# A spatial gate with one bias product per pair of heads, inverse steps placed among the vector engine's other work, and row turns one tile later

## The reference, cut to what matters

```python
def spatial_gating(u, v, ln_g, ln_b, w_s, b_s):
    v = layer_norm(v, ln_g, ln_b).reshape(b_, n, A_CHUNK, A_HEADS, HEAD_DIM)
    w = jnp.where(mask, w_s, 0.0)                    # 4 heads, 128 x 128, lower triangle
    z = jnp.einsum('hij,bnjhd->bnihd', w, v) + b_s.T[:, :, None]
    return u * z.reshape(b_, t, A_WIDTH_2)

def gated_delta_rule(q, k, v, log_g, beta):          # 8 heads, chunks
    sol = lax.linalg.triangular_solve(eye + lower, rhs, left_side=True, lower=True, unit_diagonal=True)
    ...                                              # then a recurrence over the chunks

def gla_chunked(q, k, v, log_a):                     # 4 heads, chunks of 64
    o_intra = jnp.einsum('bhnij,bhnjv->bhniv', p_intra, v)
    ...                                              # plus a state carried from chunk to chunk
```

## Time and profile before

| | us |
|---|---|
| median of 3 runs (3999.33 to 4000.17) | 3999.43 |
| the profiled execution | 3998.43 |
| its span, first to last instruction | 3996.6 |
| PE busy | 3807.0 (95% of the span) |
| DVE busy | 2082.7 (52%) |
| ACT busy | 1382.5 (35%) |

### The profile page before, as it was taken

One profiled execution on the slowest core, in us unless ns is written; L12 is line 12 of the kernel. 1 busy time (PEld: TensorE's weight loads), 2 busy tenths in 40 slices (PEclk: granted clock), 3 DMA queues, 4 the chain that ended last, 5 costly groups with the idle time before them and its releaser, 6 DMA issues.

```text
span 3996.6 us, 44618 instructions
## 1 busy us (share of the span) xinstructions
PE 3807.0 (95%) x18516; PEld 3137.8 (79%) x18516; DVE 2082.7 (52%) x3673; ACT 1382.5 (35%) x2100; POOL 86.4 (2%) x164
## 2 busy tenths in 40 slices
PE   8998989999999999999999988999999999899998
PEld 5975489999986688888887766888788877577886
DVE  5936757644456543333347467433633374756335
ACT  5434533212356432322226424222322255233222
POOL 0100001111000000000000000000000000000000
PEclk9998999999999999999999958999999999679999
DMA  6410014433320122232222201222222222002222
GB/s 225 151 43 1 1 43 132 125 127 127 103 69 22 43 95 95 99 109 100 96 95 81 78 1 43 95 95 97 85 100 95 96 84 81 15 33 85 95 99 81
DMA packets 92877, 333.35 MB, mean 83 GB/s; under 512 B 11362, under 2 KB 11522, under 8 KB 92420
## 3 DMA queue, kind: packets, MB, share of 16 engines
q1 hardware_dynamic: 77040, 278.10, 20.2%
q0 software_dynamic: 12800, 41.95, 3.4%
q10 hardware_dynamic: 2836, 10.44, 0.7%
HBM read 328.35 MB, written 2.10 MB: 83 GB/s over the span
## 4 chain that ended last, share of the span: by engine, by line
PE 89%; DVE 5%; ACT 5%; issue 1%; DMA 0%; DVEq 0%; ACTq 0%; SPq 0%
PE PS L511 73%; PE PS L1078 2%; PE PS L513 2%; PE PS L1063 1%; PE PS L1094 1%; PE PS L1066 1%; PE PS L1424 1%; PE PS L944 0%; PE PS L2372 0%; PE PS L2168 0%; PE PS L1395 0%; PE PS L716 0%; PE PS L1995 0%; ACT XH L891 0%; DVE H_r L680 0%
## 5 line engine op out<-in xcount | busy, mean ns | idle before, releaser
L511 PE MATMUL PS<-arena_r,ring_hi 128*128 128x512 f32 (+1 forms) x6224 | 2106.0, 377 | 71.2 <-DVE H_r L680 70.1
L511 PE MATMUL PS<-arena_r,ring_r 128*128 128x512 f32 (+1 forms) x4752 | 1781.4, 375 | 0.0
L511 PEld LDWEIGHTS PS<-arena_r,ring_hi 128*128 128x128 f32 x6224 | 1168.4, 189 | 253.3 <-DVE H_r L680 61.9
L511 PE MATMUL PS<-H_r,ring_hi 128*128 128x512 f32 (+1 forms) x3280 | 1231.3, 375 | 0.0
L511 PEld LDWEIGHTS PS<-arena_r,ring_r 128*128 128x128 f32 x4752 | 897.6, 189 | 131.9
L380 DVE TENSOR_TENSOR ring_r<-ring,ring_hi 128x1024 fp32r<-128x1024 f32 x514 | 627.7, 1222 | 660.5 <-ACT ring_hi L371 660.0
L371 ACT ACTIVATE ring_hi<-ring 128x1024 fp32r<-128x1024 f32 x514 | 541.9, 1056 | 875.3 <-DMA ring<-weights_dram 867.5
L511 PEld LDWEIGHTS PS<-H_r,ring_hi 128*128 128x128 f32 x3280 | 622.9, 190 | 95.5 <-issue 3.1
L1654 ACT ACTIVATE arena<-PS 128x512 f32<-128x512 f32 x88 | 52.7, 598 | 532.6 <-PE PS L511 532.6
L1232 DVE SCALAR_TENSOR_TENSOR XH<-PS,mods,XH 128x256 f32<-128x256 f32 (+1 forms) x144 | 68.5, 524 | 237.3 <-PE PS L511 237.3
L1658 DVE SCALAR_TENSOR_TENSOR arena<-arena,PS 128x512 f32<-128x512 f32 x88 | 60.5, 688 | 225.8 <-PE PS L511 225.8
(11 more groups left out here) (370 smaller groups left out, 3164.2 us busy)
## 6 DMA issues: line engine op xcount, KB each, us to landing
ring<-weights_dram SPq DMA_DIRECT2D x526, 512.0 KB, 3.2
rstd<-ada_later_dram POOLq DMA_DIRECT2D x54, 256.0 KB, 2.9
mean<-ada_later_dram POOLq DMA_DIRECT2D x53, 256.0 KB, 3.0
ada_extra<-ada_later_dram POOLq DMA_DIRECT2D x53, 256.0 KB, 3.0
XH<-xT_dram ACTq DMA_DIRECT2D x1, 3072.0 KB, 20.2
ring<-weights_dram ACTq DMA_DIRECT2D x4, 512.0 KB, 4.1
out_dram<-XH SPq DMA_DIRECT2D x8, 256.0 KB, 2.0
con<-second_dram ACTq DMA_DIRECT2D x1, 1536.0 KB
```

The source lines that it names most:

```text
L511: ins = pe.matmul(PS[:, o.bank, 0:hi - lo], w[:, 0, :], x, **flags)
```

## The change

In the projection, the turn of the gate rows and all that hangs behind it move one tile later. In the gate, the bias of the two heads of a pair is added by one product over two rows and all four chunks, ahead of the pair's head products; these follow in an order in which the two heads of a pair, which write the lower and the upper half of the same bank, alternate. In DVE's list the masking of the weights moves to the front, the inverse's steps 0 to 6 move ahead of the scaling of v, and steps 18 to 23 move behind the masks; DVE waits for its own turn of the diagonal blocks. The bias is loaded as two rows of 256.

```diff
@@ in_plan
-            t[14]["beside_pe"] = lambda pe: turn_rows_pe(pe, l)
-            t[15]["beside_act"] = lambda act: (turned_rows_act(act), high_rows_act(act))
-            t[16]["beside_pe"] = lambda pe: turn_keys_pe(pe, l)
-            t[17]["beside_dve"] = lambda dve: (key_rows_dve(dve, l), low_rows_dve(dve))
-            t[19]["beside_pe"] = lambda pe: turn_values_pe(pe, l)
-            t[20]["beside_dve"] = value_rows_dve
+            t[15]["beside_pe"] = lambda pe: turn_rows_pe(pe, l)
+            t[16]["beside_act"] = lambda act: (turned_rows_act(act), high_rows_act(act))
+            t[17]["beside_pe"] = lambda pe: turn_keys_pe(pe, l)
+            t[18]["beside_dve"] = lambda dve: (key_rows_dve(dve, l), low_rows_dve(dve))
+            t[20]["beside_pe"] = lambda pe: turn_values_pe(pe, l)
+            t[21]["beside_dve"] = value_rows_dve
@@
+        PAIR = con2_r[:, SELP:SELP + P].bitcast(F32)
@@ units_pe
-            for h in range(4):
-                o = 64 * (h % 2)
+            for q in range(2):
+                pe.matmul(PS[:, q, :].rearrange("p (n t) -> p n t", n=NLT), PAIR[0:2], bs_row[0:2, P * q:P * q + P].unsqueeze(1).to_broadcast([2, NLT, P]),
+                          start=True, stop=False, skip_group_check=True)
                 for n in range(NLT):
-                    dst = PS[o:o + 64, h // 2, P * n:P * n + P]
-                    pe.matmul(dst, vt(n, slice(64 * h, 64 * h + 64)), wsT[:, h, :], start=True, stop=False)
-                    ins = pe.matmul(dst, C("ones")[0:1, 0:64], bs_row[0:1, P * h:P * h + P], start=False, stop=True)
+                    for j in range(2):
+                        h = 2 * q + j
+                        ins = pe.matmul(PS[64 * j:64 * j + 64, q, P * n:P * n + P], vt(n, slice(64 * h, 64 * h + 64)), wsT[:, h, :],
+                                        start=False, stop=True, skip_group_check=True)
@@ solve_dve
+            mask_w_dve(dve, l)
             dve.wait_ge(so_d.sem, so_d.next("dve", 4))
-            nc.vector.transpose(LD, D_.rearrange("p q (j t) -> p t q j", j=8)).then_inc(so_ld.sem, 1)
+            ins = nc.vector.transpose(LD, D_.rearrange("p q (j t) -> p t q j", j=8))
+            ins.then_inc(so_ld.sem, 1)
+            dve.wait_ge(so_ld.sem, so_ld.next("dve"))
             centre_v_dve(dve)
+            rows_dve_of_inverse(dve, 0, 2)
             gla_decay_dve(dve)
-            mask_w_dve(dve, l)
+            rows_dve_of_inverse(dve, 2, 7)
             norm_v_dve(dve, l)
             gla_products_dve(dve)
-            rows_dve_of_inverse(dve, 0, 10)
+            rows_dve_of_inverse(dve, 7, 12)
             gla_states_dve(dve)
-            rows_dve_of_inverse(dve, 10, 24)
+            rows_dve_of_inverse(dve, 12, 18)
             sgu_out_dve(dve)
             gla_mask_dve(dve)
-            rows_dve_of_inverse(dve, 24, 31)
+            rows_dve_of_inverse(dve, 18, 31)
@@ third_loads
-                act.dma_start(bs_row[0:1, :], sgub_d[l:l + 1]).then_inc(small_loaded.sem, 16)
+                act.dma_start(bs_row[0:2, 0:2 * P], sgub_d[l].rearrange("(q j t) -> j q t", q=2, j=2)).then_inc(small_loaded.sem, 16)
```

## The result

The changed kernel takes 3976.77 us (median of 4 runs, 3973.86 to 3978.42) against 3999.38 us before: ratio 0.9945, 95% interval 0.9933 to 0.9957, 22.6 us less. The forecast was 3978.5. The span of the profiled execution went from 3996.6 to 3974.0 us. In the kernel after, lines of the gate and the solve stage stand 1 to 7 further down (the GLA's outputs are L1994, its scores L1987, the gate's head products L1980, its bias products L1975, the inverse's steps L2323 and L2325). A few executions of several of the kernels here are about 17 us shorter in the first block, which the change does not touch (the profiled one of the run with the heads in turn is such, at a granted clock of 0.96 from 300 to 600 us against 0.87 in the kernel after, so only stretches in it are compared), and one execution of the turns alone took 7779.7 us, which no trace here explains and its ratio leaves out.

A forecast was written before the change was run, and what follows sets the result against it. PE held 89% of the chain's end; in the solve stage DVE's queue set when the masks are done, PE the end from there. 2.8 + 9.4 + 8.7 = 20.9 us off 3998.4 gave 3977.5, median 3978.5; range 3971 to 3985.

The forecast's parts named there:

- The projection: Row turn one tile later: PE's wait falls from 4.5 to 3.2 us, now for the slab's low part; 1.4 us gain per layer.
- DVE's list, layer 1: Solve stage: steps 0 to 6 (4.3 us) become free, steps 18 to 23 (5.1) move behind the masks; masks end 9.4 us earlier.
- Layer 0: Solve stage of layer 0: state updates end later, at 2338.7; outputs start at 2353.15 in place of 2361.83, 8.7 us gain.
- PE's gate: Two bias products and eight pairs take 9.4 us at the low clock, 4.7 at the high, in place of 16.6.
- What is late next: After the masks, PE's outputs are last by 1.4 us over DVE's turns; the block inverse starts 9.4 us earlier.
- The pairs do run side by side: Rival, chance 0.10: gate pairs do not run side by side; gate 12.1 us, 6.6 us less in both layers, 3985.
- The recurrence did not slow down: Rival "slower", chance 0.04: recurrence after the block inverse left at 1.2 GHz, each layer pays 15 us, 4008.
- The clock did not come back sooner: Rival, chance 0.16: TensorE granted 2.4 GHz in the outputs and after the projection's wait; together 6 us more, 3972.5.
- The sum: Whole kernel: projection 2.8, layer 1's solve stage 9.4 and layer 0's 8.7 give 20.9 us gain; chance 0.64.

## Why the prediction was right, point by point

- **The projection.** Forecast: the wait falls from 4.5 to 3.2 us, the clock falls behind it as before, 1.4 us gain in each layer. The wait is 3.2, to the tenth, and released by what was named. The clock fell, but the loss behind it was mis-sized: 2.9 us in layer 1 in place of 1.6. So 1.5 us were gained in layer 0 and 0.2 in layer 1, not 1.4 twice, and the run without the turns shows that this cannot be told from nothing.
- **DVE's list, layer 1.** Forecast 9.4 us, found 9.3; steps 0 to 6 fit into the wait for the roots (0.6 us of it is left; 0.4 was forecast).
- **Layer 0.** Forecast 8.7, found 9.6. The term that was off is the end of the state updates, taken from the row of before at 3.75 us; after, they took 1.96, at the high clock. Nothing in my forecast called for that, so it is luck: in the run without the turns layer 1 has them at 3.75, so that 8.1 us are gained there and not 9.3.
- **PE's gate.** I went by the upper bound of 9.4 us. It took 4.2 (3445.42 to the end of the second eight), even below the lower bound of 4.7, at a granted clock of 1.00. It changed nothing in the sum, as PE waits 5.5 us for the masks; and at 0.50, in the run without the turns, it took 7.8 and was covered too, as the forecast had it.
- **What is late next.** Outputs last by 1.4 us over DVE's first turn: they end at 3472.65, the turn at 3471.28. Shown by the run with steps 16 and 17 moved, where 1.8 us at the outputs became 1.3 at the block inverse.
- **The rivals.** The pairs do run side by side, and at the high clock it would not have mattered: the rival's price of 6.6 us assumed 0.52 us for a head product, which was the mean of the old gate over alternating shapes and both clocks (0.36 and 0.62). The recurrence did not slow down: from the start of layer 1's outputs to the end of the span it is 513.9 us, 514.8 before. The clock did not come back sooner: in the outputs PE is busy 11.88 of 12 us at 0.50. If a busy engine in the records is taken for activity, this trace again does not agree with the Trainium skill's rule (TensorE: Matmul & The Clock Gate, Part 1) that sustained activity releases the clock.
- **The sum.** 20.9 us was forecast, 22.6 found between the two spans. 1.4 of the difference is the form stage of layer 0, which was no term of mine: the granted clock is 1.00 from 2299.2 to 2302.6 there, where it was 0.50 from 2291.2 to 2311.7 before. The change does not touch that stage, and the runs differ there (25.9 us with the turns alone, 26.8 before, 27.2 with the gate alone), so I take it for chance. Layer 0 gave 0.9 more than forecast and the projection 1.1 less: the time came nearer to the forecast than its terms did.

## What to carry to other kernels

Where two engines are each nearly late at the same join, price an edit of one by the time at which the other gets there: DVE's order alone brought 1.5 us, the gate alone 0.3, both together 18 to 19. Before moving a step off a waiting engine's path, look at the very next thing that it will ask for and at who makes that, in the program order of the maker: here both the turn and the next slab hung on the same stretch of ACT, and only moving both helped (6 us a layer). An fp32 product of a single row between others was not cheap here: a head product and its one-row product took 0.72 us together at 2.4 GHz, a head product in a run of its own shape 0.19. So add a bias in a run of its own, over as many columns as one product takes.

## What the runs showed that I had not expected

A shorter wait did not leave TensorE slow for less: behind 3.2 us the changed kernel has 7 products at the low clock's pace in layer 0 and 13 in layer 1, behind 4.5 us the kernel before has 8 and 9. So shortening a wait without ending it can gain nothing. And an edit in the projection showed in the solve stage: where the state updates got 1.2 GHz, DVE waited 1.7 to 1.8 us for them, and the outputs came 1.2 to 2.1 us later. Lastly, products of one shape in a row went at 0.19 us where the same products between one-row ones took 0.36 at the same clock.
